# Residual stream with the tokens in the partitions, norms as sums along rows

## The chip, the cores and the metric

The program runs on one core of a Trainium2 chip. The metric is the device time of one execution in microseconds (us). Engines: PE (TensorE), DVE (VectorE), ACT (ScalarE), POOL (GpSimd) and SP, whose queue here only issues DMAs.

## The reference

Two blocks are chained on one sequence of 1024 tokens with 1024 features, in fp32. The residual stream `h` (then `x`) is changed six times, each time by the same form, a matrix product whose rows (tokens) are normed and added:

```python
# first block
z = rms_norm(h, g_mix_pre) @ w_in                 # attention heads and pooled windows
h = h + rms_norm(mix @ w_out, g_mix_post)
hn = rms_norm(h, g_ffn_pre)
ff = (silu(hn @ w_ffn_gate) * (hn @ w_ffn_up)) @ w_ffn_down
h = h + rms_norm(ff, g_ffn_post)
e = rms_norm(p @ w_ple_proj, g_ple)
h = h + sigmoid(h @ w_ple_gate) * e
# second block: layer a (recurrent heads), then layer b (differential attention)
for l in range(2):
    proj = rms_norm(x, pre_norm[l]) @ w_in[l]
    ...
    y = concatenate([y_br * silu(gate), y_mem * silu(g_mem)]) @ w_out[l]
    x = x + rms_norm(y, post_norm[l])

def rms_norm(x, g):      # over the 1024 features of a token
    return x * rsqrt(mean(x * x, axis=-1) + 1e-6) * g
```

## The kernel before

Each fp32 operand of a product is held as a rounded high part and a low part, and each product of 128x128 by 512 is three matmuls: high by high, high by low, low by high (L725 to L727 in `Product`, whose output has features in the partitions and tokens along the row; L777 to L779 in `TokenProduct`, tokens in the partitions; L1469 to L1471 in `Down`, two units instead of eight). One `Product` is 8 units, so 24 matmuls and one 128x512 bank of PSUM.

The residual stream `k.x` lies with features in the partitions (`KT` = 8 tiles of 128 features by 1024 tokens). A norm's sum over features thus runs across partitions. It is made of squares (ACT, L920 or L1167), added into one 128x512 tile (DVE, L930 or L1185), then summed over partitions and spread again by a matmul with ones (`Rsqrt`, L583), with Ln and Exp on ACT (L590, L592). The result `r` is a 128x512 tile that multiplies every later tile: y by r (L1175), the embedding by r (`ScaleEmbedding`), and the outputs of the next layer's products in their evictions (`EvictHidden` L1431 and L1433, `EvictNormed`, `EvictShift`, `EvictStore`).

The output layers (`w_out` in the mixer and in layers a and b, `w_ple_proj`, `w_ple_gate`) are `Product`s in two passes (`two_passes`): eight tiles of features for the first 512 tokens, then the same eight in reverse for the second 512. Weights come in pieces of 128x1024 (512 KB) into a ring of four slots; for each, SP issues the load, POOL multiplies a gain where there is one (L671), and a `Round` makes the high part on ACT (L685) and the low part on DVE (L690). Four of eight pieces are still in the ring when the second pass starts, the other four are loaded again. `chain` runs beside the second pass of an output layer: y times r (L1175), x plus y (L1188 on DVE, L1148 on POOL), high part (L1162), square (L1167), low part (L1151 on POOL, L1179 on DVE), sum of squares (L1185); `RowRstd` (L1570) makes the same `r` for tokens in partitions. The steps of the second half of tokens (`k.late`) run beside the first products of the next layer.

x is brought into features-in-partitions by `TurnX` (L3166, 8 transposes for 128 tokens) while the mixer's `w_out` runs, and brought back by `Store` at the end of the program (L1617 on PE, L1625 on ACT, L1632 on DVE, then a 512 KB DMA per 128 tokens).

The program is one list of steps. A step issues what it has on each of the five queues, and each queue runs in the list's order; `weave(main, (at, steps), ...)` puts steps before main product number `at`, and `with_weights` places each piece's load, gain and round: the load after the step that last used its slot, the gain and the round one to three products ahead of the first use. Nothing is reordered at run time: an engine waits for the semaphores of its next instruction.

In time: the mixer's attention ends and its `w_out` starts at 420.8 us, the feed-forward (FFN) runs to 1283.8, the last group of `Down` and the embedding product (PLE) to 1370.1, the PLE gate and the first products of layer a follow; layer a's recurrence lies between about 1530 and 2260, its `w_out` ends its first pass at 2313.9, layer b's at 3013.3.

## Time and profile before

| | before |
|---|---|
| median of 3 runs | 3091.33 us (3088.25 to 3096.96) |
| profiled execution: span | 3091.6 us |
| PE busy | 2780.4 us (90%), 20842 matmuls |
| DVE busy | 1609.7 us (52%), 2838 instructions |
| ACT busy | 1058.3 us (34%), 2056 instructions |
| POOL busy | 642.1 us (21%), 483 instructions |
| DMA | 162.46 MB, mean 53 GB/s |

The span is the time from the first to the last instruction of one profiled execution. Its own time is taken as that span: it differs from the median of the runs by 0.3 us, less than the runs differ among themselves. Busy PE time counts matmuls as the profile models them; a pipelined matmul is 0.39 us long, but the next starts before it ends.

### The profile page before, as it was taken

The page shows a single profiled execution, that of the slowest core. Times are in us where ns is not written, and L with a number is a line of the kernel's source. Part 1 is how long each engine was busy: PE and PEld are TensorE (multiplying, and loading weights), DVE is VectorE, ACT ScalarE, POOL GpSimd, SP SyncE. Part 2 cuts the span into 40 slices and gives each one's busy share as a digit, 9 for nine tenths or more (in the row PEclk, how much of TensorE's full clock was granted, in tenths as well). Part 3 has the DMA queues.
Part 4 walks back from the last instruction along what each step waited for, and adds up shares of the span by engine and source line. Part 5 has one row for each costly group of instructions (what it writes and reads, how often), then busy time and mean ns, then how long its engine had stood idle before and what let it go on. Part 6 is the DMA issues. An engine that isn't in the chain of part 4 may idle for free.

```text
span 3091.6 us, 50154 instructions
## 1 busy us (share of the span) xinstructions
PE 2780.4 (90%) x20842; PEld 2216.5 (72%) x20842; DVE 1609.7 (52%) x2838; ACT 1058.3 (34%) x2056; POOL 642.1 (21%) x483
## 2 busy tenths in 40 slices
PE   7998988799999999879999988888887999999877
PEld 6775666588888888757788855878766778766555
DVE  3426675444444444477555416777455433477744
ACT  4216744311111111353222122444444222254552
POOL 2104243211011011054211101222113202122113
PEclk9999999899999999989999996999988999999988
DMA  3111041011111111112211210000122201010042
GB/s 103 52 48 55 15 136 55 29 53 48 41 55 48 48 48 48 48 48 83 76 39 36 65 56 2 4 31 4 44 95 82 75 14 57 28 38 32 29 148 83
DMA packets 200322, 162.46 MB, mean 53 GB/s; under 512 B 5232, under 2 KB 173850, under 8 KB 199586
## 3 DMA queue, kind: packets, MB, share of 16 engines
q1 hardware_dynamic: 200098, 159.26, 16.4%
q8 instruction: 167, 2.74, 0.4%
q14 instruction: 57, 0.47, 0.0%
HBM read 137.19 MB, written 22.05 MB: 52 GB/s over the span
## 4 chain that ended last, share of the span: by engine, by line
PE 76%; DVE 10%; ACT 5%; issue 4%; POOL 3%; DMA 2%; SPq 0%; DVEq 0%; ACTq 0%; POOLq 0%
PE ps L725 16%; PE ps L726 15%; PE ps L727 15%; PE ps L2417 7%; PE ps L1822 3%; PE ps L1899 2%; PE ps L1469 2%; PE ps L1470 2%; PE ps L1471 2%; DVE r L690 1%; PE ps L1913 1%; PE ps L777 1%; PE ps L779 1%; PE ps L778 1%; ACT r L685 1%
## 5 line engine op out<-in xcount | busy, mean ns | idle before, releaser
L725 PE MATMUL ps<-r,r 128*128 128x512 f32 (+1 forms) x2304 | 939.2, 408 | 100.0 <-DVE r L690 58.9
L726 PE MATMUL ps<-r,r 128*128 128x512 f32 (+1 forms) x2304 | 909.5, 395 | 0.0
L727 PE MATMUL ps<-r,r 128*128 128x512 f32 (+1 forms) x2304 | 908.3, 394 | 0.0
L725 PEld LDWEIGHTS ps<-r,r 128*128 128x128 f32 x2304 | 443.2, 192 | 232.9 <-DVE r L690 67.2
L671 POOL TENSOR_TENSOR sb<-sb 128x1024 f32<-128x1024 f32 x138 | 279.1, 2027 | 1287.8 <-DMA sb<-in_w_ffn_up 481.4
L726 PEld LDWEIGHTS ps<-r,r 128*128 128x128 f32 x2304 | 443.5, 192 | 94.5 <-issue 8.2
L727 PEld LDWEIGHTS ps<-r,r 128*128 128x128 f32 x2304 | 442.3, 192 | 94.3
L690 DVE TENSOR_TENSOR r<-sb,r 128x1024 fp32r<-128x1024 f32 x198 | 271.4, 1378 | 227.8 <-ACT r L685 227.5
L2417 PE MATMUL ps<-sb 64*64 64x64 f16 (+2 forms) x8832 | 269.5, 217 | 33.0 <-issue 12.4
L2417 PEld LDWEIGHTS ps<-sb 64*64 64x64 f32 (+1 forms) x8832 | 254.1, 127 | 56.5 <-issue 37.9
L685 ACT CAST r<-sb 128x1024 fp32r<-128x1024 f32 x198 | 204.9, 1043 | 213.0 <-POOL sb L671 212.9
L1421 ACT CAST r<-sb 128x512 fp32r<-128x512 f32 x44 | 27.3, 620 | 383.7 <-DVE sb L1436 383.7
L1469 PE MATMUL ps<-r,r 128*128 128x512 f32 x352 | 138.7, 394 | 8.7 <-DVE sb L1482 7.4
L1846 DVE CUSTOM_DVE_ANT_0 sb<-ps,sb 128x128 f32<-128x128 f32 (+7 forms) x160 | 120.9, 756 | 32.5 <-PE ps L1899 15.9
L1470 PE MATMUL ps<-r,r 128*128 128x512 f32 x352 | 137.1, 389 | 0.0
L1471 PE MATMUL ps<-r,r 128*128 128x512 f32 x352 | 137.1, 389 | 0.0
L1863 ACT ACTIVATE sb<-sb 128x128 f32<-128x128 f32 (+7 forms) x160 | 123.1, 772 | 36.9 <-DVE sb L1849 36.4
L1482 DVE TENSOR_TENSOR sb<-sb,ps 128x512 f32<-128x512 f32 x160 | 106.1, 684 | 54.6 <-PE ps L1471 54.6
L930 DVE TENSOR_TENSOR sb<-sb 128x512 f32<-128x512 f32 x70 | 63.5, 907 | 111.3 <-ACT sb L920 100.3
L1822 PE MATMUL ps<-sb 64*128 64x512 f32 (+2 forms) x480 | 102.0, 529 | 4.8 <-DVE sb L1846 2.4
L1151 POOL TENSOR_TENSOR r<-sb,r 128x512 fp32r<-128x512 f32 x44 | 68.8, 1571 | 172.0 <-ACT r L1162 172.0
L1433 DVE TENSOR_TENSOR ps<-ps,sb 128x512 f32<-128x512 f32 x44 | 30.8, 699 | 138.4 <-PE ps L727 138.4
(273 smaller groups left out, 3609.2 us busy)
## 6 DMA issues: line engine op xcount, KB each, us to landing
sb<-in_w_out SPq DMA_DIRECT2D x36, 512.0 KB, 3.9
sb<-in_a_w_in SPq DMA_DIRECT2D x29, 512.0 KB, 3.7
sb<-in_w_ffn_gate SPq DMA_DIRECT2D x22, 512.0 KB, 3.9
sb<-in_w_ffn_up SPq DMA_DIRECT2D x22, 512.0 KB, 3.7
sb<-in_w_ffn_down SPq DMA_DIRECT2D x22, 512.0 KB, 3.4
sb<-in_w_in SPq DMA_DIRECT2D x17, 512.0 KB, 4.1
sb<-in_x SPq DMA_DIRECT2D x16, 512.0 KB, 5.5
xs<-sb SPq DMA_DIRECT2D x4, 2048.0 KB, 9.4
```

The costliest lines, as they stand in the source:

```text
L671: pool.tensor_tensor(w.raw, w.raw, w.gain.unsqueeze(2).broadcast_to((P, w.nk, w.n)), ALU.mult).then_inc(*s.w_gain.up(w.id))
L685: act.copy(w.hi, w.raw).then_inc(*s.w_hi.up(w.id))
L690: dve.tensor_tensor(w.lo, w.raw, w.hi.bitcast(F32), ALU.subtract).then_inc(*s.w_lo.up(w.id))
L725: pe.matmul(self.out, w.hi[:, q, self.cols], hi, start=(q == 0), stop=False)
L726: pe.matmul(self.out, w.hi[:, q, self.cols], lo, start=False, stop=False)
L727: ins = pe.matmul(self.out, w.lo[:, q, self.cols], hi, start=False, stop=(q == w.nk - 1))
L1469: pe.matmul(self.out, w.hi[:, 0, cols], hi, start=(q == 0), stop=False)
L1470: pe.matmul(self.out, w.hi[:, 0, cols], lo, start=False, stop=False)
L1471: ins = pe.matmul(self.out, w.lo[:, 0, cols], hi, start=False, stop=(q == 1))
L1822: ins = pe.matmul(k.banks(2 * h)[:, b:b + m], of.q(i)[o, iq * P:(iq + 1) * P], of.keys(i)[o, b:b + m], start=True, stop=True)
L1863: act.activation(sc, sc, ACT.Exp, bias=s4[:, 1:2], accum_out=s4[:, 2:3]).then_inc(*s.exped.up((of.id, i, iq, h)))
L2417: ins = pe.matmul(self.bank(b + p // n, n, w)[o, p % n, :], lhs[o, p], rhs[o, p], start=(j == 0 and not onto and not (keep and p)), stop=( ...
```

## The change

The residual stream is kept with tokens in the partitions: `k.x` is `ST` = 8 tiles of 128 tokens by 1024 features.

- Every output layer is a `TokenProduct` per 128 tokens (`j`) and 512 output features (`c`), still 24 matmuls. `EvictRows` squares the bank on ACT with a sum along the row (a 128x1 column), and DVE moves it out times the gain, a 128x1024 row broadcast to all partitions and loaded by one DMA per output layer. `RowSum` adds the two halves' sums (DVE, 128x1) and POOL takes the power -0.5 of a 128x1 column. `RowAdd` is one DVE instruction on 128x1024: x + y * r.
- For the next layer, `RowSquare` squares the new row of x on ACT with its sum, POOL makes the 128x1 factor (scale and power) and multiplies the row by it (128x1024); `TurnRow` turns it by 8 transposes on PE, `SplitRow` makes the high part (ACT) and the low part (DVE), 128x1024 each. So the operand of the next layer is already normed, and `r` is gone from the evictions of all layers.
- In the FFN's last group, `FfnRow` sums squares on ACT, and POOL multiplies y by the gain row (128x1024) before `RowAdd`; the PLE gate's sigmoid is made on ACT, times e on POOL (128x512), and added by `RowAdd`.
- Weights of `w_out` and of the PLE gate are loaded once, 8 pieces of 2x512 columns (512 KB), which stay through both halves of the tokens; `Ring` lists extra places in SBUF that serve as slots for that time.
- `TurnX` and `Store` are gone: x is loaded in rows (two DMAs of 2 MB at the mixer's end), and each finished row of x goes out by a DMA of its own at the end.

Counts over the program, before and after: 128x128 transposes on PE +128, ones-matmuls of 128x512 -16, 128x1 matmuls of `RowRstd` -16; DVE 2838 to 2610 instructions, ACT 1822 to 1600 as the program issues them, POOL 485 to 534 (64 of them powers of a 128x1 column, 24 row scalings of 128x1024 with one input, 4 more two-input multiplications of 128x1024, 44 multiplications of 128x512 by `r` gone); rounds of weights 198 to 182; DMAs on SP 308 to 287.

```diff
+class RowSum(Step):
...
+    def dve(self, dve):
+        s, of, j, stat = self.s, self.of, self.j, self.stat
+        dve.wait_ge(*s.row_sq.at((of.id, j, 1)))
+        dve.scalar_tensor_tensor(stat[:, 2:3], stat[:, 0:1], D * EPS, stat[:, 1:2], ALU.add, ALU.add).then_inc(*s.row_sum.up((of.id, j)))
+
+    def pool(self, pool):
+        s, of, j, stat = self.s, self.of, self.j, self.stat
+        pool.wait_ge(*s.row_sum.at((of.id, j)))
+        pool.tensor_tensor(stat[:, 3:4], stat[:, 2:3], self.k.neg_half, ALU.pow).then_inc(*s.row_pow.up((of.id, j)))
...
+class RowAdd(Step):
...
+        dve.wait_ge(*s.row_pow.at((of.id, j)))
+        x = k.x[:, j, :].rearrange("p (c n) -> p c n", c=2)
+        dve.scalar_tensor_tensor(x, of.y(j), of.stat[:, j, 3:4], x, ALU.mult, ALU.add).then_inc(*s.row_added.up((of.id, j)))
...
+class RowSquare(Step):
...
+        act.activation(self.row.row, k.x[:, j, :], ACT.Square, accum_out=of.stat[:, j, 4:5]).then_inc(*s.x_sq.up((of.id, j)))
...
+        pool.tensor_scalar(mean, ms, 1.0 / D, EPS, ALU.mult, ALU.add).then_inc(*s.row_mean.up((of.id, j)))
+        pool.wait_ge(*s.row_mean.at((of.id, j)))
+        pool.tensor_tensor(r, mean, k.neg_half, ALU.pow).then_inc(*s.row_rms.up((of.id, j)))
+        pool.wait_ge(*s.row_rms.at((of.id, j)))
+        pool.tensor_scalar(self.row.row, k.x[:, j, :], r, 1.0, ALU.mult, ALU.mult).then_inc(*s.row_normed.up((of.id, j)))
...
+class FfnRow(Step):
...
+        pool.tensor_tensor(of.y(j), of.y(j), of.gain.rearrange("p (c n) -> p c n", c=2), ALU.mult).then_inc(*s.y_gained.up((of.id, j)))
...
+def out_products(k, pieces, op, of):
+
+
+    order = [(c, j) for first in (0, 4) for c in range(2) for j in range(first, first + 4)]
+    return [TokenProduct(k, pieces[c], op, j, EvictRows(k, of), HALF, c) for c, j in order]
...
+    for j in range(ST):
+        plan.setdefault(5 + j if j < 4 else 9 + j, []).append((0, [RowSum(k, of, j)]))
+        plan.setdefault(8 + j if j < 4 else 9 + j, []).append((2, row_plan(k, of, j, keep(j), squared=turned(j))))
+        if of.rows:
+            plan.setdefault(10 + j if j < 4 else 11 + j, []).append((1, [TurnRow(k, of.rows[j]), SplitRow(k, of.rows[j])]))
...
+class EvictRows(Evict):
...
+        act.activation(of.part(j, c), st.out, ACT.Square, accum_out=of.stat[:, j, c:c + 1]).then_inc(*s.row_sq.up((of.id, j, c)))
...
+        dve.scalar_tensor_tensor(of.part(j, c), st.out, math.sqrt(D), of.gain[:, span_of(c)], ALU.mult, ALU.mult).then_inc(*s.y_rows.up((of.id, j, c)))
...
-def chain(k, ev, y, acc, second, extra=(), back=None):
...
-    chains = [residual(k, h, y=y, r=acc[h], rstd_id=norms[h].id, x_op=op, acc=r[h], alone=True) for h in range(2)]
...
+    base, ext = k.ring, (F + 8192, F + 10240, F + 14336)
+    pieces = [token_pieces(k, w_out, c * HALF, HALF, gains, only, hold) for c, only, hold in ((0, base, 0), (1, (*ext, F + 12288), 2))]
...
+    main = out_products(k, pieces, op, made)
+    plan, k.late = out_plan(k, made)
...
-            dve.tensor_tensor(g, st.out, self.r[h], ALU.mult).then_inc(*s.hidden_r.up((n, h)))
...
-    store = [Store(k, i, rows, [("x_added", (adds[i // 4][0].key, KT - 1))] if i % 4 == 0 else []) for i in range(ST)]
...
+        out = [Dma(k, to[j * P:(j + 1) * P, :], k.x[:, j, :], f"dma_out{j % 4}", [("row_added", (rows.id, j))]) for j in range(ST)]
```

Three places in the order of instructions. In its rows `L` numbers of the changed kernel are that kernel's own. First, DVE in the second half of the mixer's `w_out`, before (L930: sum of squares of y; L3182: turned x copied; L1175, L1188: y times r, x plus y; L1185: sum of squares of x; L690: a weight's low part):

```order
L930 TENSOR_TENSOR sb<-sb 128x512
L3182 COPY sb<-ps 128x4x128
L1175 TENSOR_TENSOR sb<-sb 128x512
L1188 TENSOR_TENSOR sb<-sb 128x512
L1175 TENSOR_TENSOR sb<-sb 128x512
L1185 TENSOR_TENSOR sb<-sb 128x512
L1188 TENSOR_TENSOR sb<-sb 128x512
L690 TENSOR_TENSOR r_1024_80<-sb,r_1024_81 128x1024
```

and after (L1039: y out of the bank times the gain; L603: sum of the halves' squares; L626: `RowAdd`; L574: low part of a turned row; L853: a weight's low part, here of the FFN's first pieces):

```order
L1039 SCALAR_TENSOR_TENSOR sb<-ps,sb 128x512
L603 SCALAR_TENSOR_TENSOR sb<-sb 128x1
L574 TENSOR_TENSOR r_8192_67<-ps,r_8192_66 128x8x128
L626 SCALAR_TENSOR_TENSOR sb<-sb 128x1024
L1039 SCALAR_TENSOR_TENSOR sb<-ps,sb 128x512
L603 SCALAR_TENSOR_TENSOR sb<-sb 128x1
L626 SCALAR_TENSOR_TENSOR sb<-sb 128x1024
L853 TENSOR_TENSOR r_1024_74<-sb,r_1024_75 128x1024
L853 TENSOR_TENSOR r_1024_76<-sb,r_1024_77 128x1024
L853 TENSOR_TENSOR r_1024_78<-sb,r_1024_79 128x1024
L853 TENSOR_TENSOR r_1024_80<-sb,r_1024_81 128x1024
L1039 SCALAR_TENSOR_TENSOR sb<-ps,sb 128x512
```

What stood between the second pass's weights as two to four instructions on 128x512 is one on 128x1024 a row, and the low parts of the next layer's first four weights stand in one block behind it.

Second, DVE in the FFN's last group of `Down`, before (L1482: `Down` added to y; L1538: low part of the turned embedding input):

```order
L1482 TENSOR_TENSOR sb<-sb,ps 128x512
L930 TENSOR_TENSOR sb<-sb 128x512
L1482 TENSOR_TENSOR sb<-sb,ps 128x512
L930 TENSOR_TENSOR sb<-sb 128x512
L1538 TENSOR_TENSOR r_1024_64<-ps,r_1024_56 128x512
L1538 TENSOR_TENSOR r_1024_65<-ps,r_1024_57 128x512
```

and after (L1522 is `Down` added to y):

```order
L1522 TENSOR_TENSOR sb<-sb,ps 128x512
L574 TENSOR_TENSOR r_8192_67<-ps,r_8192_66 128x8x128
L1522 TENSOR_TENSOR sb<-sb,ps 128x512
L626 SCALAR_TENSOR_TENSOR sb<-sb 128x1024
L1522 TENSOR_TENSOR sb<-sb,ps 128x512
L574 TENSOR_TENSOR r_8192_67<-ps,r_8192_66 128x8x128
L1522 TENSOR_TENSOR sb<-sb,ps 128x512
L626 SCALAR_TENSOR_TENSOR sb<-sb 128x1024
```

A sum of squares per bank becomes a row's add and a low part per two banks. On POOL the same stretch, which held nothing of the `Down` group before, has behind the FFN's gains (L834) for each row

```order
L834 TENSOR_TENSOR sb<-sb 128x1024 x40
L683 TENSOR_SCALAR sb<-sb 128x1
L684 TENSOR_TENSOR sb<-sb 128x1024
L686 TENSOR_TENSOR sb<-sb 128x1
L683 TENSOR_SCALAR sb<-sb 128x1
```

that is the mean, the multiplication by the gain row, and the power, ahead of each `RowAdd`.

Third, the program's end on DVE, before:

```order
L690 TENSOR_TENSOR r_1024_74<-sb,r_1024_75 128x1024
L930 TENSOR_TENSOR sb<-sb 128x512
L1632 COPY sb<-ps 128x512 x2
L930 TENSOR_TENSOR sb<-sb 128x512
L1632 COPY sb<-ps 128x512 x2
L930 TENSOR_TENSOR sb<-sb 128x512
L1175 TENSOR_TENSOR sb<-sb 128x512 x8
L1632 COPY sb<-ps 128x512 x4
```

and after:

```order
L1039 SCALAR_TENSOR_TENSOR sb<-ps,sb 128x512
L603 SCALAR_TENSOR_TENSOR sb<-sb 128x1
L626 SCALAR_TENSOR_TENSOR sb<-sb 128x1024
L1039 SCALAR_TENSOR_TENSOR sb<-ps,sb 128x512
L603 SCALAR_TENSOR_TENSOR sb<-sb 128x1
L626 SCALAR_TENSOR_TENSOR sb<-sb 128x1024
```

The eight multiplications and four copies behind the last product's sum are gone; one sum and one `RowAdd` stand behind its eviction.

## Rows read from the trace of the kernel before

**Rows 1.** Page: chain that ended last; costliest group (busy, mean | idle).

```profile
PE 76%; DVE 10%; ACT 5%; issue 4%; POOL 3%; DMA 2%; SPq 0%; DVEq 0%; ACTq 0%; POOLq 0%
...
L725 PE MATMUL ps<-r,r 128*128 128x512 f32 (+1 forms) x2304 | 939.2, 408 | 100.0 <-DVE r L690 58.9
```

**Rows 2.** Busy time by stretch: engines, clock, DMA share, GB/s.

```profile
421.00:633.00 212.00, 175.05 (x718) 138.39 (x718) 111.63 (x125) 83.99 (x133) 62.35 (x34) 0.90 0.22 70
1284.00:1370.00 86.00, 56.05 (x215) 41.94 (x214) 54.45 (x69) 54.84 (x88) 20.47 (x14) 0.84 0.13 39
1370.00:1521.00 151.00, 137.61 (x581) 110.40 (x580) 105.02 (x111) 54.59 (x82) 70.92 (x41) 0.98 0.26 83
2314.00:2442.00 128.00, 101.96 (x407) 80.16 (x408) 61.54 (x72) 44.27 (x72) 37.35 (x21) 0.89 0.27 87
```

**Rows 3.** PE's waits, 421 to 633 us: total, times, longest.

```profile
PE ps L725 <- DVE r L690: 24.5, 7, 5.8
```

**Rows 4.** PE's waits, 1284 to 1370 us.

```profile
PE ps L583 <- DVE sb L930: 19.4, 3, 9.2
PE ps L725 <- DVE r L1538: 6.7, 1, 6.7
```

**Rows 5.** PE's waits, 1370 to 1521 us.

```profile
PE ps L725 <- DVE r L690: 13.4, 6, 3.6
```

**Rows 6.** PE's waits, 2314 to 2442 us.

```profile
PE ps L725 <- DVE r L690: 11.6, 3, 5.5
PE ps L1570 <- DVE sb L1185: 11.0, 2, 8.3
```

**Rows 7.** L725's matmuls, 656.0 to 699.7 us: durations, first and last start.

```profile
L725 PE MATMUL ps<-r,r x64: 389/389/389, 656.1 to 698.9; 128*128 128x512 f32 x64
```

**Rows 8.** Timeline of PE around one turned tile: start, duration.

```profile
450.55 1.04 PE L3166 MATMUL ps<-sb 128*128 128x128 f32 x8
451.35 0.50 PE L725 MATMUL ps<-r,r 128*128 128x512 f32 x1
...
456.91 0.49 PE L3166 MATMUL ps<-sb 128*128 128x128 f32 x3
```

**Rows 9.** A weight's low part on DVE: alone (group), and beside POOL.

```profile
L690 DVE TENSOR_TENSOR r<-sb,r 128x1024 fp32r<-128x1024 f32 x4 | 4.8, 1221 | 4.6 <-ACT r L685 4.6
...
3028.93 3.84 POOL L1148 TENSOR_TENSOR sb<-sb 128x512 f32<-128x512 f32 x2 [24.68 <-DVE sb L1175]
...
3029.31 2.31 DVE L690 TENSOR_TENSOR r<-sb,r 128x1024 fp32r<-128x1024 f32 x1
```

**Rows 10.** Groups of 1284 to 1370 us on DVE.

```profile
L930 DVE TENSOR_TENSOR sb<-sb 128x512 f32<-128x512 f32 x28 | 26.4, 944 | 25.2 <-ACT sb L920 14.3 <-ACT sb L1494 10.4
...
L1482 DVE TENSOR_TENSOR sb<-sb,ps 128x512 f32<-128x512 f32 x16 | 10.8, 679 | 0.0
```

**Rows 11.** DMA issues by tensor, KB, median us to landing.

```profile
sb<-in_w_out SPq DMA_DIRECT2D x36, 512.0 KB, 3.9
...
out<-sb SPq DMA_DIRECT2D x8, 512.0 KB, 2.8
```

**Rows 12.** Groups of POOL: a weight's gain, and its smallest copy.

```profile
L671 POOL TENSOR_TENSOR sb<-sb 128x1024 f32<-128x1024 f32 x138 | 279.1, 2027 | 1287.8 <-DMA sb<-in_w_ffn_up 481.4 <-DMA sb<-in_a_w_in 262.4 <-DMA sb<-in_w_in 147.7
...
L2604 POOL COPY sb<-sb 128x6 f32<-128x6 f32 x16 | 3.2, 200 | 0.0
```

**Rows 13.** Timeline of the end, engines apart.

```profile
3014.74 0.50 PE L725 MATMUL ps<-r,r 128*128 128x512 f32 x1 [1.27 <-ACT sb L921]
...
3063.38 0.39 PE L727 MATMUL ps<-r,r 128*128 128x512 f32 x1
...
3067.73 11.29 DVE L1175 TENSOR_TENSOR sb<-sb 128x512 f32<-128x512 f32 x8 [2.60 <-ACT sb L592]
...
3068.57 12.80 POOL L1148 TENSOR_TENSOR sb<-sb 128x512 f32<-128x512 f32 x8 [19.49 <-DVE sb L1175]
...
3081.42 6.38 PE L1617 MATMUL ps<-sb 128*128 128x128 f32 x32 [15.11 <-POOL sb L1148]
```

More of the change, by code:

```diff
@@ L722, in pe @@
         for q in units:
-            x.wait(pe, s, q, self.h)
+            x.wait(pe, s, q, self.span.start)
             hi, lo = x.hi[q][:, self.span], x.lo[q][:, self.span]
@@ L3215, in feed_forward @@
         prods = [Product(k, ws[i], x, hidden, i, h) for i, h in order]
-        yield from weave(prods, *(late if p == 0 else [(2, down)]))
+        yield from weave(prods, *(late if p == 0 else [(2, down)]), *([(6, gain_rows)] if p == 1 else []))
         wd = [Weights(k, w_down[:, 2 * p + q:2 * p + q + 1, :], 1, D) for q in range(2)]
-        down = [Down(k, wd, hidden, y, p, o, h, squares if p == last else None) for h in range(2) for o in range(KT)]
-    rows = k.at(k.XL + 4 * S, ST, PLE)
-    pt = Operand(k.hi[6:8], k.lo[6:8], None)
@@ L3221, in feed_forward @@
[L3221 to L3227 removed]
+        down = [Down(k, wd, hidden, y, p, j, c, (2 * j + c) % 4 if p == last else None) for j in range(ST) for c in range(2)]
@@ L3337, in finish_layer @@
                      (3, [norm.end(1, parts[1]), norm.begin(1, range(4, BT)), *two[2:4]]), (4, [norm.end(1, parts[2]), *two[4:6]]),
-                     (5, two[6:8]), (6, two[8:]), (7, back[1:]))
-    if layer == 0:
-        yield from chain(k, ev, y, acc, second, back=[st.event() for st in back])
-        return
-    norms = [Rsqrt(k, acc[h], acc[h], 4 + h, D, ev.summed(h)) for h in range(2)]
-    adds = [residual(k, h, y=y, r=acc[h], rstd_id=norms[h].id) for h in range(2)]
-    rows = k.at(F + 8192, 4, D)
@@ L3345, in finish_layer @@
-    store = [Store(k, i, rows, [("x_added", (adds[i // 4][0].key, KT - 1))] if i % 4 == 0 else []) for i in range(ST)]
-    there = [After(k, pool=[st.event()]) for st in back]
-    yield from weave(second, (1, [norms[0], there[0]]), *by(2, adds[0], 2), (6, store[:2]), (7, store[2:4]))
-    yield from [norms[1], there[1], *adds[1], *store[4:]]
+                     (5, two[6:8]), (6, two[8:]), (7, back), *plan)
+    yield Ring(k, base)
+    k.xs, k.rows = Operand(tiles_of(row_hi), tiles_of(row_lo), None if layer else rows.ready), rows
@@ L3351, in layer_b @@
+    if layer:
+        for _, steps in k.late:
+            yield from steps
+        yield After(k, sp=[out[j].event() for j in range(4, ST)])
 def layer_b(k):
```

756 lines of the change are left out of this document (313 added, 443 removed).

## The prediction

> **What bounds the kernel now.** I read the page's chain first: 76% of the span runs through PE and 10% through DVE, and the costliest group, L725, stood idle 100.0 us, 58.9 of them for a weight's low part (L690) [rows 1]. So PE is the bound, and what the change can take is PE's idle time around the norms and what runs when PE has nothing to do. I then read one undisturbed FFN stretch for the price of a product: 64 first matmuls of three start over 42.8 us, 0.679 us for three, so 5.44 us for a product of 24 [rows 7]. Then the busy time by stretch, to see how much longer each output layer is than its products [rows 2], and PE's waits in each [rows 3 to 6]. Last, the end of the program, where no product is left [rows 13].
>
> The mixer's output and FFN entry, 421 to 633 us, hold 26 products (208 matmuls of L725), 141.4 us at 5.44, and 8 turned tiles. One of these costs 0.92 us: 6.36 from one turn's start to the next, less 5.44 [rows 8]. That is 148.8 of 212.0 us, so 63 us go to norms, waits and the slower clock after stalls (mean 0.90) [rows 2]. Of the waits, 24.5 are for L690 [rows 3]. The last group of FFN and the embedding, 1284 to 1370, has PE busy 56.1 of 86 us at clock 0.84 [rows 2], and waits 19.4 for the sum of squares (L930) and 6.7 for the turned embedding input [rows 4]. The PLE gate stretch, 1370 to 1521, waits 13.4 for L690 [rows 5]. Layer a's second pass with layer b's first products, 2314 to 2442, waits 11.6 for L690 and 11.0 for L1185 in `RowRstd` [rows 6]. Behind the last matmul at 3063.4 come 28 us in which DVE, then POOL (12.80), then PE's turns follow one another [rows 13].
>
> **The change, part by part.** The matmuls of the products stay. Each output layer gets 8 groups of 8 transposes where x must be an operand again, 0.92 each [rows 8].
>
> *Mixer, 421 to 633.* Products 141.4, turns 7.4 (in place of `TurnX`'s, which are as many). Of the six norms by ones-matmuls, the two of attention and pool that stay I leave at 6 with their waits. The weights of `w_out` are loaded once, and lie there from the first products on, so in the second half nothing waits for L690; these rounds were late because each stood on DVE behind the chain's instructions on 128x512. The first product of `w_out` still waits: its piece can be loaded only once the last products of the kv weights free a slot, and then come load 3.9 [rows 11], gain 2.0 [rows 12], and a cast and a low part on as many elements, 1.2 each where nothing contends [rows 9], 8.3 us, against less than a product of cover, so 5. The FFN's first four low parts stand in one block on DVE behind their gains on POOL, 4 x 2.0 = 8.1 us after a load of 3.9, ahead of the eviction of product 13; PE has four banks, three products ahead of it, so this is hidden, but at the edge: 8 us for it and for a lowered clock (bounds: 0, and the 24.5 that L690 costs now). Sum 168, against 212: -44 (bounds -52 and -28).
>
> *FFN.* The periods are full of matmuls already [rows 7]. Its evictions lose one DVE pass; PE doesn't wait for them, so nothing.
>
> *Last `Down` group and embedding.* The squares on banks (28 x 0.944 = 26.4 us of DVE [rows 10]) and the turned halves go. A row now takes on DVE two `Down` adds (2 x 0.68 [rows 10]), a `RowAdd` and a low part on 128x1024, each between 1.22 and 2.31 [rows 9]: 3.8 to 6.0, nearest 4.1, since the low part reads PSUM. On POOL a row takes the gain (two inputs, 128x1024), 2.0 as the weight's gain [rows 12] to 3.8 as two contended 128x512 [rows 9], and two small ones. The first `RowAdd` can start about 12 us in (four `Down`s, square, gain, power). Then 8 x 4.1 = 33, then the 16 embedding products of 6 matmuls, 16 x 1.36 = 22, and 4 for what they drag. 71 against 86: -15 (bounds: 57, PE's busy time, -29; and 86, 0).
>
> *PLE gate.* 24 products 130.6, turns 7.4; the eight weight pieces are loaded once, so of 13.4 us waiting for L690 [rows 5] I leave 4: 142 against 151, -9 (bounds -13 and 0).
>
> *Layer a.* 16 products 87.0 and turns 7.4; the 11.0 before `RowRstd`, which made the products behind it wait, and the 11.6 of the second pass go [rows 6]; x comes back from DRAM by two DMAs that can start only behind the last split and stand close ahead of the first add. I leave 4.6 for them: 99 against 128, -29 (bounds -34 and -20).
>
> *Layer b and the end.* Without its wait of 1.27, the product that starts at 3014.74 would have followed at 3013.3, 0.17 before the last matmul's modelled end [rows 13]. Eight products more are 43.5 us, to 3056.8. Behind the last one stand: square and sum of its bank on ACT and the move on DVE, each like a pass over a bank, 0.7 [rows 10], a 128x1 sum and power, each at least the 0.2 of the smallest POOL copy [rows 12], `RowAdd` 1.3 [rows 9], and the DMA out, 2.8 [rows 11], with the hops 7.5 in all. The end is then 3064.3 against 3091.6: -27. The other row's power and add are done by then, since rows come 5.44 us apart and cost DVE some 3. Gone with it are the 11.29 of L1175, 12.80 of L1148 and 6.38 of turns [rows 13].
>
> *Small things.* Four vector loads fewer at the start against one or two more rounds ahead of the mixer's output: nothing. Gain rows are loaded early.
>
> Sum: -44 -15 -9 -29 -27 = -124. The profiled execution's span is 3091.6, its own time, 0.3 from the median of the runs: **2967 us**.
>
> **One price no row shows** is POOL's power on a 128x1 column, 64 times. The nearest rows are its 128x6 copy at 0.20 [rows 12], the least, and the gain of 128x1024 at 2.0 [rows 12] for a whole tile. I take 0.3, nearest the small one. At 2.0 a row takes 4.0 more on POOL; POOL is busy 62 of 212 us [rows 2], so this stays hidden except at the end, where it adds 1.7.
>
> **Two rules weighed.** DVE's low part took 2.31 us beside POOL's add and 1.22 without it [rows 9]: they hold each other up. The Trainium skill, SBUF — State Buffer, section "SBUF: two separate sides", says that a GpSimd instruction and a DVE instruction with two SBUF inputs exclude each other for the whole instruction. `RowAdd` is such an instruction, and POOL's row gain would stand in its way in the PLE stretch. By the row, `RowAdd` is 2.3 at worst and the sum moves by 8; by the rule, it is the second rival below. The rule of the page GPSIMD Engine Reference, section "Engine selection", that a two-input pass is about twice as slow on GpSimd speaks against `FfnRow`'s multiplication there; the rows agree in kind, 2.0 against 1.22 [rows 9, 12], and the sum has it.
>
> **Rivals.** *Forecast* (2950 to 2985): 0.55. *DVE and POOL take turns*: in the last `Down` group, in the gate stretch and at the head of each output layer, a `RowAdd` waits for a whole POOL instruction. 8 rows x 3 us (between 2.0 and 3.8 [rows 9, 12]) in the `Down` stretch alone: 2991 (2985 to 3010); for it speaks 2.31 against 1.22, against it that DVE has slack in all other stretches (111.6 busy of 212 [rows 2]): 0.23. *The waits for L690 stay*, since the rounds still stand in DVE's order behind evictions that wait for ACT: 24.5 + 13.4 + 11.6 = 49.5 [rows 3, 5, 6] and half as much again for the clock, which stood at 0.90 and 0.89 in these stretches [rows 2]: 2967 + 75 = 3042 (3010 to 3060). For it speaks that the block of four low parts is in line ahead of an eviction; against it that twelve loads became eight in each output layer: 0.12. *The power is slow* (the other side): POOL carries 8 rows x 2 powers in each of four stretches, 64. At 6 us a power, a row takes 14.4 of POOL against two products, 10.9: 28 us late a stretch, four times 112, and in mixer and layer a the gains of 16 pieces, 2.0 each [rows 12], queue behind it, 64 more: 2967 + 176 = 3143. It ends slower than now from 5.2 us a power on. Nothing in the profile is near it (0.2 for a copy [rows 12]), but no row shows it: 0.05. *Better than forecast* (below 2950): 0.05, if the `Down` stretch falls to PE's 57.
>
> **How the numbers follow.** 2967 is the likeliest case's. The range, 2945 to 3015, takes the second rival in and most of the forecast's bounds, and leaves out 0.17 or so, most of the third rival and the fourth. What a measurement of this kernel can tell from no change is 0.3%, 9 us. Faster by more: all but the slow power and half a case of lost gains, 0.92; within: 0.03; slower: 0.05.
>
> **What the changed profile would show.** PE's waits from 421 to 590 us under 25 us in all and the FFN entry shorter by 44; no wait for a sum of squares in the PLE stretch; its `RowAdd` near 1.3 to 2.3 us; after layer a's first pass 16 products in 99 us; less than 8 us behind the last matmul; POOL's power well under 1 us. The prediction is wrong if the L853 rows still release PE for tens of microseconds, if POOL is what `RowAdd` waits for at every row, or if a power takes microseconds.

## The result, and the profile after

The changed kernel takes 2963.09 us (median of 4 runs, 2959.86 to 2970.36) against 3089.79 for the kernel before, measured again beside it (4 runs): ratio 0.9593, 95% interval 0.9576 to 0.961. The forecast was 2967 us. The profiled execution has a span of 2958.6 us, 133.0 less than that of before; the medians differ by 126.7, so some 6 us of what follows is spread between executions.

The page of the profile after, the chain that ended last and the costliest groups (L888 is `Product`'s first matmul now, L943 `TokenProduct`'s):

```profile
PE 81%; DVE 7%; POOL 3%; ACT 3%; issue 3%; DMA 2%; SPq 0%; DVEq 0%; ACTq 0%; POOLq 0%
...
L888 PE MATMUL ps<-r,r 128*128 128x512 f32 (+1 forms) x1760 | 699.9, 398 | 9.1 <-DVE r L853 5.1
...
L943 PE MATMUL ps<-r,r 128*128 128x512 f32 (+1 forms) x768 | 303.6, 395 | 55.4 <-ACT r L1431 27.8
```

It answers to [rows 1]: PE's share of the chain rose from 76 to 81%, and the idle time ahead of the first matmuls of a product fell from 115.0 us (100.0 on L725, 15.0 on L777, the first of `TokenProduct` before) to 64.5 (9.1 and 55.4). Of it, waits for a weight's low part fell from 73.9 us (58.9 and 15.0) to 26.4 (5.1 and 21.3). L777's row of before, and the changed kernel's largest wait for weights over the whole program:

```profile
L777 PE MATMUL ps<-r,r 128*128 128x512 f32 (+1 forms) x224 | 81.1, 362 | 15.0 <-DVE r L690 15.0
...
PE ps L943 <- DVE r L853: 21.3, 7, 6.7
```

The stretches of [rows 2], in the changed kernel's times (start and end, length; then PE, PEld, DVE, ACT, POOL busy, clock, DMA share, GB/s), and the end:

```profile
417.00:587.00 170.00, 155.58 (x696) 126.81 (x697) 79.13 (x85) 61.60 (x105) 56.78 (x50) 0.97 0.21 72
1238.00:1308.00 70.00, 57.99 (x276) 47.02 (x275) 50.59 (x68) 35.87 (x68) 33.41 (x32) 0.93 0.19 63
1308.00:1449.00 141.00, 138.06 (x641) 114.49 (x640) 45.46 (x56) 35.22 (x50) 50.60 (x48) 1.00 0.20 66
2239.00:2341.00 102.00, 97.02 (x452) 80.44 (x452) 40.18 (x44) 29.38 (x49) 33.81 (x36) 0.98 0.24 78
...
2952.00:2959.00 7.00, 0.32 (x2) 0.00 (x0) 2.04 (x3) 0.69 (x2) 0.55 (x1) 0.90 0.27 111
```

The same 26, 24 and 16 products fit in 170, 141 and 102 us instead of 212, 151 and 128, at a clock of 0.97, 1.00 and 0.98 instead of 0.90, 0.98 and 0.89. DVE fell from 111.6 to 79.1 us of the first, from 105.0 to 45.5 of the third stretch. The table has the times between the same products in both traces, in us, from start of matmul to start of matmul. There is one exception: for the ninth `w_out` product of layers a and b, the column of before takes the end of the eighth (2313.9 and 3013.3), as the forecast did. The ninth itself started 1.3 us later in both, so by starts alone the last four changes are -4.1, -26.0, -3.8 and -26.9.

| stretch | before | after | change | forecast |
|---|---|---|---|---|
| start to the mixer's first `w_out` product | 420.8 | 416.9 | -4.0 | 0 |
| to the first `Down` (26 products) | 211.9 | 169.5 | -42.5 | -44 |
| FFN, to its last group of `Down` | 651.0 | 651.8 | +0.8 | 0 |
| `Down` and embedding, to the PLE gate | 86.4 | 69.5 | -16.9 | -15 |
| 24 products from the gate on | 151.1 | 141.3 | -9.8 | -9 |
| to layer a's ninth `w_out` product | 792.7 | 789.9 | -2.8 | 0 |
| 16 products from there | 128.5 | 101.3 | -27.2 | -29 |
| to layer b's ninth `w_out` product | 570.9 | 568.5 | -2.4 | 0 |
| to the end | 78.3 | 50.0 | -28.3 | -27 |

What such a difference is worth is seen where the code is the same. In the changed kernel and in e3, e6 and e7 below, four short stretches took the same time to 0.1 us wherever the edit didn't touch them: first `w_out` product to first `Down` (169.4 to 169.5), PLE gate (141.3 to 141.4), layer a's 16 products (101.3), the end (50.0). The start up to the kv products took 379.8 to 383.4 us, and the long stretch to layer b's ninth product 568.5 to 574.9. Two profiles of the kernel before, its own and e10's (the same code but for the last layer), differ more: 382.8 and 378.9 for the start, 572.3 and 575.0 for the long stretch, 151.1 and 148.3 for the PLE gate. (The kv products are small ones for the memory's keys and values, the last ahead of the mixer's `w_out`.)

PE's waits, 417 to 587 us and 1238 to 1308, in the changed kernel (total, times, longest), which answer to [rows 3, 4]:

```profile
PE ps L943 <- DVE r L853: 7.7, 2, 6.7
PE ps L551 <- issue: 5.0, 2, 4.5
PE ps L742 <- DVE sb L783: 1.8, 1, 1.8
...
PE ps L551 <- DVE r L1565: 6.0, 2, 4.8
PE ps L943 <- DVE sb L1039: 5.6, 2, 4.0
```

L853 is the low part of a weight, L551 a row's transposes, L1565 the turned embedding input, L1039 a bank moved out. No wait for the sum of squares of y or x is left; the 1.8 us (L742) are of a norm of the mixer's operand, which stays. The 24.5 us for weights are 7.7, of which 6.7 stand inside the first `w_out` product, after its first six matmuls. The 5.0 before the turns are new.

The wait of 6.7 us is for the second piece of `w_out`. Its way through the engines (timelines; L1417 and L1420 are the operand's own split on DVE, L1431 its cast on ACT):

```profile
415.63 5.17 POOL L834 TENSOR_TENSOR sb<-sb 128x1024 f32<-128x1024 f32 x2
...
418.97 2.38 DVE L1420 TENSOR_TENSOR r<-sb,r 128x512 fp32r<-128x512 f32 x1
...
421.99 0.62 ACT L1431 CAST r<-sb 128x512 fp32r<-128x512 f32 x1 [2.29 <-DVE sb L1417]
...
423.85 4.06 DVE L853 TENSOR_TENSOR r<-sb,r 128x1024 fp32r<-128x1024 f32 x2 [1.30 <-ACT r L848]
```

Its load was issued at 404.51, and POOL started its gain at 415.63 without waiting for the load. Then the cast stood on ACT behind the split's cast, which came late since two of DVE's passes of 128x512 took 2.38 us each beside POOL's gains, instead of 0.68. So this wait comes from the order, not from a slot in the ring. The last piece, whose load was issued at 416.16 when the last kv product had freed its slot, cost the other 1.0 us.

The end, engine by engine (timeline):

```profile
2951.94 0.39 PE L945 MATMUL ps<-r,r 128*128 128x512 f32 x1
...
2952.36 0.60 ACT L1032 ACTIVATE sb<-ps 128x512 f32<-128x512 f32 x1 [4.75 <-PE ps L945]
...
2953.15 0.69 DVE L1039 SCALAR_TENSOR_TENSOR sb<-ps,sb 128x512 f32<-128x512 f32 x1 [2.65 <-ACT sb L1032]
...
2953.99 0.55 POOL L608 TENSOR_TENSOR sb<-sb 128x1 f32<-128x1 f32 x1 [4.89 <-DVE sb L603]
...
2954.65 1.28 DVE L626 SCALAR_TENSOR_TENSOR sb<-sb 128x1024 f32<-128x1024 f32 x1 [0.74 <-POOL sb L608]
...
2955.96 0.33 SPq L1583 DMA_DIRECT2D out<-sb  x1
```

Square, move, sum, power (0.55), `RowAdd` (1.28) and one store follow the end of the last matmul in 6.3 us, where 27.8 stood (28.2 from its start [rows 13]).

Where the new wait before the turns comes from, POOL, DVE and PE in the mixer (timelines):

```profile
511.98 7.47 POOL L834 TENSOR_TENSOR sb<-sb 128x1024 f32<-128x1024 f32 x4
519.40 0.55 POOL L608 TENSOR_TENSOR sb<-sb 128x1 f32<-128x1 f32 x1
...
512.02 1.87 DVE L603 SCALAR_TENSOR_TENSOR sb<-sb 128x1 f32<-128x1 f32 x1
520.07 1.29 DVE L626 SCALAR_TENSOR_TENSOR sb<-sb 128x1024 f32<-128x1024 f32 x1 [6.17 <-POOL sb L608]
523.57 5.47 DVE L853 TENSOR_TENSOR r<-sb,r 128x1024 fp32r<-128x1024 f32 x4 [2.21 <-ACT r L848]
...
526.93 1.55 PE L551 MATMUL ps<-sb 128*128 128x128 f32 x8 [4.54 <-issue]
```

The FFN's first four gains stand on POOL in one block; a row's power (L608) waits behind them, `RowAdd` 6.17 us for it, then four low parts come in one block on DVE, and PE idles 4.54 us before the turn. Layer a has the same hole (4.6 us).

The last `Down` group, 1238 to 1308 us, by groups:

```profile
L684 POOL TENSOR_TENSOR sb<-sb 128x1024 f32<-128x1024 f32 x8 | 21.8, 2726 | 0.6
...
L1522 DVE TENSOR_TENSOR sb<-sb,ps 128x512 f32<-128x512 f32 x16 | 10.5, 680 | 0.3 <-PE ps L1511 0.3
L626 DVE SCALAR_TENSOR_TENSOR sb<-sb 128x1024 f32<-128x1024 f32 x8 | 10.2, 1280 | 4.3 <-POOL sb L686 4.3
...
L686 POOL TENSOR_TENSOR sb<-sb 128x1 f32<-128x1 f32 x8 | 5.4, 674 | 0.0
```

A row takes POOL 4.1 us at first, 2.4 to 3.3 for the gain of y and 0.55 for the power, and the first three `RowAdd`s start 4.1 us apart. The later ones don't: 7.8, 4.4, 3.9, 8.0 and 3.5 us lie between them. Ahead of the fourth, the row's power was ready 3.8 us early. DVE had the turned embedding input's low parts (L1565) behind the third `RowAdd`, PE idled 4.8 us for them before its next turn, and DVE then waited 2.57 us for that turn's cast. The other gap of 8 us also has the embedding input's low parts in it.

### The profile page after: what moved, and what is told of

It is laid out like the page before. It is cut to its first block, busy times and chain, and to the rows that moved or that the text cites. A ratio compares the mean times of both kernels' runs of the same rounds, so it can differ in the third digit from the quotient of the medians.

```text
span 2958.6 us, 49843 instructions
## 1 busy us (share of the span) xinstructions
PE 2739.6 (93%) x20906; PEld 2198.7 (74%) x20906; DVE 1410.7 (48%) x2610; ACT 954.2 (32%) x1930; POOL 603.3 (20%) x532
## 4 chain that ended last, share of the span: by engine, by line
PE 81%; DVE 7%; POOL 3%; ACT 3%; issue 3%; DMA 2%; SPq 0%; DVEq 0%; ACTq 0%; POOLq 0%
PE ps L888 14%; PE ps L890 13%; PE ps L889 13%; PE ps L2359 7%; PE ps L943 5%; PE ps L945 5%; PE ps L944 5%; PE ps L1764 3%; PE ps L1509 2%; PE ps L1511 2%; PE ps L1510 2%; PE ps L1841 2%; PE ps L1855 1%; DVE r L853 1%; PE ps L1872 1%
## 5 line engine op out<-in xcount | busy, mean ns | idle before, releaser
L888 PE MATMUL ps<-r,r 128*128 128x512 f32 (+1 forms) x1760 | 699.9, 398 | 9.1 <-DVE r L853 5.1
L890 PE MATMUL ps<-r,r 128*128 128x512 f32 (+1 forms) x1760 | 685.5, 390 | 0.0
L889 PE MATMUL ps<-r,r 128*128 128x512 f32 (+1 forms) x1760 | 685.3, 389 | 0.0
L834 POOL TENSOR_TENSOR sb<-sb 128x1024 f32<-128x1024 f32 x134 | 269.8, 2023 | 1230.6 <-DMA sb<-in_w_ffn_up 484.2
L888 PEld LDWEIGHTS ps<-r,r 128*128 128x128 f32 x1760 | 333.3, 189 | 101.2 <-issue 24.1
L853 DVE TENSOR_TENSOR r<-sb,r 128x1024 fp32r<-128x1024 f32 x182 | 240.3, 1336 | 315.4 <-ACT r L848 315.1
L890 PEld LDWEIGHTS ps<-r,r 128*128 128x128 f32 x1760 | 332.9, 189 | 69.4
L889 PEld LDWEIGHTS ps<-r,r 128*128 128x128 f32 x1760 | 333.4, 189 | 65.6 <-issue 1.5
L943 PE MATMUL ps<-r,r 128*128 128x512 f32 (+1 forms) x768 | 303.6, 395 | 55.4 <-ACT r L1431 27.8
L945 PE MATMUL ps<-r,r 128*128 128x512 f32 (+1 forms) x768 | 294.7, 384 | 0.0
L944 PE MATMUL ps<-r,r 128*128 128x512 f32 (+1 forms) x768 | 294.4, 383 | 0.0
L848 ACT CAST r<-sb 128x1024 fp32r<-128x1024 f32 x182 | 187.0, 1045 | 266.3 <-POOL sb L834 241.5
L943 PEld LDWEIGHTS ps<-r,r 128*128 128x128 f32 x768 | 148.3, 193 | 94.3 <-issue 43.8
L945 PEld LDWEIGHTS ps<-r,r 128*128 128x128 f32 x768 | 148.3, 193 | 28.1
L944 PEld LDWEIGHTS ps<-r,r 128*128 128x128 f32 x768 | 148.7, 194 | 27.3 <-issue 1.9
```

What stands on the lines that cost most here:

```text
L834: pool.tensor_tensor(w.raw, w.raw, w.gain.unsqueeze(2).broadcast_to((P, w.nk, w.n)), ALU.mult).then_inc(*s.w_gain.up(w.id))
L853: dve.tensor_tensor(w.lo, w.raw, w.hi.bitcast(F32), ALU.subtract).then_inc(*s.w_lo.up(w.id))
L888: pe.matmul(self.out, w.hi[:, q, self.cols], hi, start=(q == 0), stop=False)
L889: pe.matmul(self.out, w.hi[:, q, self.cols], lo, start=False, stop=False)
L890: ins = pe.matmul(self.out, w.lo[:, q, self.cols], hi, start=False, stop=(q == w.nk - 1))
L943: pe.matmul(self.out, hi, w.hi[:, j, :], start=(q == 0), stop=False)
```

## The experiments

Ratios are to the kernel before, run on the same chip. Most of what is compared is a stretch of one profile, between the same products; how much such stretches differ with the same code is said above. "kv stretch" is that from the kv products to the first `Down`: 250.0 us before, 203.1 after.

**e1: w_out loaded and split again.**

```diff
+    again = [[Weights(k, w.src, w.nk, w.n, w.gain, w.only) for w in ws] for ws in pieces]
-    return [TokenProduct(k, pieces[c], op, j, EvictRows(k, of), HALF, c) for c, j in order]
+    return [TokenProduct(k, (again if j > 3 else pieces)[c], op, j, EvictRows(k, of), HALF, c) for c, j in order]
```

> Changed kernel, but the eight pieces of w_out are loaded, multiplied and split again for the second half of the tokens, in the mixer and in layers a and b: 24 loads and 24 rounds more. Theory (the wait for low parts went because the chain's passes left DVE, not because there are fewer rounds): DVE was busy 79 of 170 us in the mixer stretch and 40 of 102 in layer a's, so the 24 rounds fit in and cost 2 to 8 us in all, ratio to the kernel before 0.960 to 0.962. Rival (the saved rounds carry the gain): at least a third of the 69 us gained in the two stretches comes back, over 20 us, ratio above 0.966.

Measured: 0.9658 (0.9645 to 0.9671), 21 us more in the profile, 14.6 of them in the kv stretch (217.7). The whole lies at the rival's bound. In the two stretches that it names, 14.6 us and nothing (layer a's 16 products took 101.3 as before the edit) came back, more than the theory's 2 to 8 and less than the rival's 20. The extra time was one wait of 7.18 us before a turn at 494.65, one of 2.37, and the clock after them. So the count of rounds and the places of what was added had to be told apart (e5, e9).

**e2: gains and rounds of the next layer's first four pieces one product apart.**

```diff
-        ws = {i: columns(k, w[i % 2], i // 2 * P, gain=V["g_ffn_pre"]) for i in ids}
+        ws = {i: columns(k, w[i % 2], i // 2 * P, gain=V["g_ffn_pre"], hold=0 if p else i) for i in ids}
-    ws = [columns(k, w, col, gain=g) for w, col, g, _, _ in jobs]
+    ws = [columns(k, w, col, gain=g, hold=n if n < 4 else 0) for n, (w, col, g, _, _) in enumerate(jobs)]
```

> Changed kernel, but the gain and round of the next layer's first four pieces are put one product apart (FFN and layer b) instead of in one block of four. Theory (the block of four gains on POOL, 7.5 us, keeps a row's power waiting, so RowAdd, and the low parts in one block keep the eviction and turn waiting; PE idles 5.0 us there in the mixer and 5.0 in layer a, and the next product runs 1.5 us slower at the lowered clock): both holes close, 10 to 13 us less, ratio 0.955 to 0.956. Rival (the hole comes from the turns themselves, or moves to the first FFN product's weights): less than 3 us.

Measured: 2951.01 us, 0.9568 (0.9555 to 0.9581). The kv stretch is 197.2 us (-5.9) and layer a's, from its first `w_out` product over 24, 158.8 instead of 163.1 (-4.3). The hole closed to this row of PE's timeline:

```profile
534.02 1.06 PE L551 MATMUL ps<-sb 128*128 128x128 f32 x8 [1.66 <-issue]
```

The theory holds for both places, 10.2 us. The parts that repeat best give the same: 164.5 us from the first `w_out` product to the first `Down` (-5.0) and 96.3 for layer a's 16 products (-5.0). Against the changed kernel's interval the two ratios only just overlap, so the whole is not as certain as its parts.

**e3: the first piece of the mixer's w_out into a place that is free earlier.**

```diff
+    for w, only in ((pieces[0][0], ext[:1]), (pieces[1][0], ext[1:2]), (pieces[1][1], ext[2:3]), (pieces[1][2], (F + 12288,)), (pieces[1][3], base)):
+        w.only = only
```

> Changed kernel, but the first piece of the mixer's w_out goes into an extra place in SBUF, free earlier, instead of the ring slot that the last kv product frees; the last piece takes that ring slot. Theory (the first product waits 6.7 us for this piece's load, gain and split, and runs at a lowered clock after it): 6 to 10 us less, ratio 0.956 to 0.958. Rival (the wait is then for the low part of the operand, or for the norm of the attention's half): less than 2 us, ratio 0.959.

Measured: 0.9592 (0.9578 to 0.9605). The kv stretch became 197.4 (-5.7), a little less than the 6 to 10 us that were expected, but the ratio doesn't show it: the stretch to layer b's ninth product, with unchanged code, was 6.4 us longer in its profile. It is a small gain in its place, not shown in the whole. The theory had the wrong piece: the 6.67 us are for the second one, as shown above. Part of the gain went into a wait that moved: in place of 6.67 us inside the first product PE idles 5.73 ahead of it.

**e4: e2 and e3 together.**

> Both of the two edits before. Theory: the gains add, 16 to 23 us less than the changed kernel, about 2943 us, ratio 0.952 to 0.954. Rival (one of them moves its wait into the other's place): no more than the better one alone.

Measured: 2952.24 us, 0.9569 (0.9553 to 0.9585); kv stretch 194.6. The gains don't add up to more than e2 alone. The fastest version that was run is thus e2 (with e4 level), some 8 us below the changed kernel by the ratios.

**e5: e1 with gains and rounds put apart**, two by two for the reloaded pieces (`hold` of `q // 2`), one by one for the next layer's.

> The reload of w_out with its 24 rounds more (which cost 21 us in one profile, 14.6 of them in the mixer), but with the gains and rounds put apart: one by one for FFN and layer b, two by two for the reloaded pieces. Theory (POOL's blocks of four gains, 7.5 to 9.4 us, and DVE's blocks of four low parts hold up the rows; the number of rounds hardly counts): the mixer stretch from the kv products on loses at most 5 us against the spread version (197 us there), ratio below 0.960. Rival (the rounds cost by their number): the stretch stays near 212 us and the ratio near 0.964.

Measured: 0.9595 (0.9566 to 0.9624). In layer a the reload costs nothing (158.8, as in e2). The kv stretch is 209.7, between the two forecasts, and holds one long wait. Rows of PE, POOL, DVE and SP of this kernel, and last the one of SP of the changed kernel:

```profile
493.57 1.94 PE L551 MATMUL ps<-sb 128*128 128x128 f32 x8 [7.91 <-issue]
...
488.87 1.28 DVE L626 SCALAR_TENSOR_TENSOR sb<-sb 128x1024 f32<-128x1024 f32 x1 [9.81 <-DMA sb<-in_x]
...
491.43 0.19 POOL L647 TENSOR_SCALAR sb<-sb 128x1 f32<-128x1 f32 x1 [11.73 <-ACT sb L641]
...
476.41 0.42 SPq L1584 DMA_DIRECT2D sb<-in_x  x1
```

```profile
466.19 0.38 SPq L1583 DMA_DIRECT2D sb<-in_x  x1
```

The first half of x is issued 10 us later, since it stands on SP behind reloaded pieces that wait for their slots, and the first `RowAdd` needs it: DVE idled 9.81 us for it. In e1 it was the same wait (8.80 us).

**e9: e5 with x ahead of those pieces on SP** (`(8, x_back[:1])` becomes `(7, x_back[:1])`).

> The last reload version (w_out loaded and split again for the second half, gains and rounds put apart), with the load of the first half of x issued ahead of the second group of reloaded pieces on SP instead of behind it. In the mixer the reload still cost 12.4 us against the spread version, and the first turn of a row waited 7.9 us there. Theory (that wait is for x, whose load stood on SP behind pieces whose slots weren't free, not for the rounds): the stretch from the kv products to the first Down falls from 209.7 to 198 to 202 us. Rival (the rounds themselves cost it): it stays above 206.

Measured: 0.9576 (0.955 to 0.9601), kv stretch 201.7, and no wait before a turn over 1.66 us. x was issued at 474.52, ahead of four loads of weights instead of behind them, and was there within 8.1 us, where it had taken up to 12.5. So e1's 217.7 us are e2's 197.2, 4.5 for eight rounds with gains (e9 less e2), 8.0 for x's place on SP's queue (e5 less e9) and 8.0 for the blocks (e1 less e5), of which the changed kernel has 5.9 itself. From the first `w_out` product to the first `Down`, which repeats better, the same steps are 164.5, 3.4, 8.1 and 8.0. With 24 rounds more than e2 the whole is level with it within the intervals.

**e6: without FfnRow's multiplication by the gain row** (`g_ffn_post` is left out of the result).

> Changed kernel without FfnRow's multiplication by the gain row on POOL (8 of 128x1024), so g_ffn_post is left out of the result. Theory (POOL paces the rows of the last Down group at 4.1 us, DVE at 3.6): the stretch from the last Down to the PLE gate's first product, 69.5 us, gets 4 to 8 us shorter, not more, since DVE comes next; ratio 0.957 to 0.958. Rival (DVE and POOL exclude each other, and DVE pays for it): 12 us or more.

Measured: 0.9588 (0.9568 to 0.9607). The stretch of 69.5 us is 66.4: -3.1, a little under the range. Without the gain the first `RowAdd` starts 2.2 us earlier and the second another 1.5, and nothing is gained behind them: from the third row on `RowAdd`s lie 7.9, 4.5, 3.9, 8.0 and 3.5 us apart, as with the gain. So POOL paces only the first rows.

**e7: the same multiplication on DVE**, ahead of `RowAdd`.

> Changed kernel with FfnRow's multiplication by the gain row moved from POOL to DVE, just ahead of RowAdd. Theory: a row then takes 4.8 us of DVE (two Down adds 0.6 each, three passes over 1024 at 1.2) against 4.1 paced by POOL now: the stretch of 69.5 us gets 2 to 7 us longer. Rival (sharing between POOL and DVE costs more than the pass on DVE): 3 us or more shorter.

Measured: 0.9605 (0.9581 to 0.9628); the stretch is 72.2: +2.7, inside the theory's range. On DVE the pass is a net cost; on POOL it is cheaper though it is slower there.

**e8: each power on POOL four times.**

```diff
+        for _ in range(3):
+            pool.tensor_tensor(k.spare_col(), mean, k.neg_half, ALU.pow)
         pool.tensor_tensor(r, mean, k.neg_half, ALU.pow).then_inc(*s.row_rms.up((of.id, j)))
```

> Changed kernel with each of POOL's 64 powers issued four times (three results go to spare columns): 1.65 us more a power at 0.55 each. Theory (POOL has room everywhere but where it paces the rows of the last Down group, and at the end): 8 x 1.65 = 13 us more in the stretch of 69.5 us, 1.7 at the end, under 3 elsewhere: +13 to +18 us, ratio near 0.964. Rival (it is hidden but for the end): +2 to +4 us. Third (each power stands in the way of PE's turns in all stretches): over 30 us.

Measured: 2994.92 us, 0.9703 (0.9677 to 0.9729), 35.5 us more in the profile: kv stretch +8.2, `Down` stretch +8.6, gate stretch +13.7, layer a +8.0, the end +1.6. Neither of the first two theories holds; the third one's size does, and its cause shows in two places. In the mixer the hole before the turn grew from 4.54 to 10.70 us:

```profile
529.16 1.94 PE L556 MATMUL ps<-sb 128*128 128x128 f32 x8 [10.70 <-issue]
```

In the gate stretch the rows come 7.43 us apart instead of 6.34 (a product and a turn). ACT, POOL and DVE there, one row (L648 squares x; L654, L657, L658, L660 mean, powers, scale; L1087 the next row's e times gate; L633 `RowAdd`):

```profile
1415.11 1.06 ACT L648 ACTIVATE sb<-sb 128x1024 f32<-128x1024 f32 x1 [4.88 <-DVE sb L633]
...
1416.34 0.19 POOL L654 TENSOR_SCALAR sb<-sb 128x1 f32<-128x1 f32 x1 [2.59 <-ACT sb L648]
1416.62 1.58 POOL L657 TENSOR_TENSOR sb<-sb 128x1 f32<-128x1 f32 x3
1418.16 0.56 POOL L658 TENSOR_TENSOR sb<-sb 128x1 f32<-128x1 f32 x1
1418.82 1.12 POOL L660 TENSOR_SCALAR sb<-sb 128x1024 f32<-128x1024 f32 x1
1419.91 1.28 POOL L1087 TENSOR_TENSOR sb<-sb 128x512 f32<-128x512 f32 x1
...
1421.22 1.29 DVE L633 SCALAR_TENSOR_TENSOR sb<-sb 128x1024 f32<-128x1024 f32 x1 [2.32 <-POOL sb L1087]
```

That is a ring: `RowAdd`, square, mean, power, scale, then the next row's e times gate behind it on POOL, for which the next `RowAdd` waits. POOL idles 2.59 us in each turn of it and still the ring sets the pace. Less the three extra powers (1.58 to 1.65) it is 5.8 us, just inside 6.34.

**e10: the kernel before, its last adds on DVE** (`alone=True` for the last layer's chain).

> The kernel before, with the adds of x and y in the last layer on DVE, behind each multiplication by r, instead of on POOL (16 instructions of 128x512). Theory (at the end DVE's multiplications and POOL's adds hold each other up, 1.41 and 1.60 us each where DVE needs 0.69 alone): 16 passes on DVE at 0.6 are done 10 us after the start, the last turns start 3 to 5 us earlier than now, at most 5 us less in all, ratio 0.998 to 1. Rival (DVE and POOL work side by side there): the end gets 5 to 10 us longer.

Measured: 0.999 (0.9979 to 1.0001). From the start of the last product's last matmul to the end it takes 25.3 instead of 28.2 us. DVE and PE there:

```profile
3059.38 0.69 DVE L1175 TENSOR_TENSOR sb<-sb 128x512 f32<-128x512 f32 x1 [2.67 <-ACT sb L592]
3060.10 0.69 DVE L1188 TENSOR_TENSOR sb<-sb 128x512 f32<-128x512 f32 x1
...
3070.15 5.62 PE L1617 MATMUL ps<-sb 128*128 128x128 f32 x32 [12.26 <-DVE sb L1188]
```

Sixteen passes on DVE alone are done in 10.7 us, less than eight there and eight on POOL side by side took (11.29 and 12.80 [rows 13]).

**e11: the kernel before, every gain and round one product earlier.**

> The kernel before, with every weight's gain and round put one product earlier in the order. Theory (its rounds are late because ACT and DVE have the chain's passes ahead of them, and an earlier place only makes DVE wait for the load or the cast instead): the time moves by less than 10 us either way. Rival (the waits for low parts, 100 us in all, are a matter of where the rounds stand, and the layout of x has little to do with them): 20 to 50 us less, ratio 0.984 to 0.994.

Measured: 1.0005 (0.9995 to 1.0015). The time is the theory's, but it is made of two parts: the output stretches gained (kv stretch 240.9, -9.1; gate 140.5, -10.6; layer a from its first `w_out` product 181.6 instead of 189.1), and the FFN's periods, full of matmuls, went from 66.1 us each to between 67.4 and 69.3, 21.5 us more in all. Two of PE's waits (total, times, longest) in this kernel, over the whole program:

```profile
PE ps L1570 <- DVE sb L1185: 43.5, 4, 15.0
...
PE ps L725 <- DVE r L690: 10.6, 5, 3.5
```

The waits for weights on L725 fell from 58.9 [rows 1] to 10.6 us (with L777's from 73.9 to 29.7), and those for the sum of squares of x rose from 15.7 to 43.5: of what the rounds gained in DVE's order, the chain lost more than half.

**e12: the same, the FFN's pieces left in their places.**

> The kernel before, with gains and rounds one product earlier as in the last experiment, except for the FFN's pieces behind its first eight products, which keep their places. In the last experiment the output stretches gained (mixer 9.1, PLE gate 10.6, layer a 7.5 us) and the FFN's periods lost 21. Theory (about 27 of the 125 us that the layout gained were a matter of where rounds stand; the rest needs DVE freed of the chain): 20 to 30 us less than before, ratio 0.990 to 0.993. Rival (what the output stretches gain here comes back elsewhere): within 8 us of before.

Measured: 3068.39 us, 0.9934 (0.9915 to 0.9954), 20 us less than before, the low end of the theory. The kv stretch is 9.6 us shorter, the gate 10.4, layer a's 16 products 5. Waits for weights are 30.8 us (L725 12.0, L777 18.8), nearly as few as the layout leaves (26.4), and again 41.3 us are waits for the sum of squares of x.

## Why the prediction was right, and where it wasn't

The time (2967 against 2963) and every stretch of the sum, cut as the forecast cut them, came out within 2 us (by starts alone, layer a's -29 was -26.0), but for three held at nothing that gave 9 us together: -4.0 up to the mixer's output, and -2.8 and -2.4 in the long stretches of layers a and b. The last two are of the size by which profiles of the same code differ. The first is not: up to the kv products the two profiles agree (382.8 and 383.2), and from there to the first `w_out` product it is 38.1 us before (38.2 to 39.0 in e10 to e12) and 33.6 after (33.7 in e6, 31.3 in e7). Before, PE waited 8.5 us there for weights' low parts, after for none; the forecast had looked at low parts only from 421 us on. Inside the stretches some prices were right by luck, as said below.

*PE's idle time was the prize.* Right: PE is busy as long as before but for 41 us (2739.6 against 2780.4, part of it fewer ones-matmuls, part matmuls no longer run at the lower clock), and the rest of the 133 us is idle time that went.

*Weights no longer late.* The forecast gave it to DVE's order: rounds stood behind the chain's passes. e11 and e12 show the order's part: one product earlier, without any change of layout, they give 20 us, about a sixth of the whole, and then the sums of squares are late in their place. The layout takes both away at once. That it does so because a norm needs no pass of its own on DVE is what e9, e11 and e12 leave, and it fits the fall of DVE's busy time; no run puts those passes back into the changed kernel's output layers, so it is not shown by itself. The forecast had called the "loaded once" part of it a cause as well; e9 against e2 shows that it counts little: 8 rounds with gains 4.5 us in the mixer, none that can be seen in layers a and b.

*"this is hidden, but at the edge"*, of the block of four gains and four low parts: it wasn't hidden. PE idled 5.0 us in the mixer, within the 8 us that the sum had left for it there, and 5.0 in layer a, where the sum had left nothing for it but 4.6 for x coming back. x cost no wait there, so that term came out by luck. e2 closed both holes. It is the eviction's neighbour that suffered, a row's power on POOL, which the forecast hadn't named.

*"The first product of `w_out` still waits"*, 5 us, for a slot, the load, the gain and the split. It was 7.7, and only 1.0 of it was for the piece whose slot came free late. The other 6.7 are the second piece's, loaded in time and then late in the order of POOL and ACT. The size was near, the reason mostly wrong.

*`Down` and embedding, 71 us.* 69.5. The forecast had DVE take 4.1 us a row, evenly. It was POOL that took 4.1 us (the gain of y alone 2.7 us on the mean), and for the first three rows only; with two gaps of 8 us the eight rows took 37 us from the first `RowAdd` to the last one's end instead of 33. Here too the sum is better than its parts. The page SBUF — State Buffer of the Trainium skill (section "SBUF: two separate sides") has a GpSimd instruction and a DVE instruction with two SBUF inputs exclude each other for the whole instruction. The trace agrees: in the mixer, a 128x1 sum on DVE that started beside the first of POOL's gains took 1.87 us instead of 0.15, as long as that gain. But the rival built on it, with `RowAdd` as the loser, was wrong in this stretch: `RowAdd` took 1.28 us there on the mean, as it is released by POOL's power and starts ahead of the next gain, and it was the gain that took 3.29 instead of 2.41:

```profile
1249.37 1.28 DVE L626 SCALAR_TENSOR_TENSOR sb<-sb 128x1024 f32<-128x1024 f32 x1 [2.17 <-POOL sb L686]
...
1249.61 3.29 POOL L684 TENSOR_TENSOR sb<-sb 128x1024 f32<-128x1024 f32 x1
```

The forecast's sign of being wrong, "if POOL is what `RowAdd` waits for at every row", didn't come as stated: DVE waited for POOL ahead of 17 of the 40 `RowAdd`s. Among them are three of the eight in the `Down` group, none of which is left in e6, and all eight in the gate stretch. There the stretch came out as forecast all the same, and e8 shows how little was to spare.

*The power, "I take 0.3 ... At 2.0 ... this stays hidden except at the end, where it adds 1.7".* This step failed. The power took 0.55 us. At 2.2 (e8) it cost 35 us, not 2. The step compared POOL's busy time with the stretch, and so did the rival of a slow power, which allowed 10.9 us a row and a break-even of 5.2 us a power. The rows of the second half come one product apart, and the power stands in a ring through three engines whose slack is 0.5 us in the gate stretch. The four stretches together lost 38 us for 1.65 a power. If that went on evenly, powers of some 6 us would use up the whole gain (an estimate from e8), near the break-even of 5.2 that was given. But the first 2 us aren't free, as the forecast had it; that the real power took 0.55 is what kept this error out of the time.

*The end.* 6.3 us stand behind the last matmul, against 7.5 forecast. The whole, -28.3, is that DVE, POOL and PE each have one row left instead of eight tiles and four turns; e10 shows that lifting the contention alone would have given 2.9 of it.

What stays open: the share of DVE's freed passes by itself; whether the long stretches of layers a and b gained anything, which one profile each doesn't tell; and how much of e3 and e4 is real.
